# Values of a gated linear attention branch: features on partitions before, tokens on partitions now

## The reference

```
u, q, k, v, r, glr, ga, gb = split(h @ w_in)       # v: 512 columns, 4 heads of 128
q, k, v, r, glr = [to_col_major(t, rows) for ...]  # latent tokens only; rows = 8
# per direction, per chunk of 64 tokens:
kv    = einsum('jd,je->de', k * exp(g_last - gc), v)
state = decay * state + kv
o     = (masked scores) @ v + (q * exp(gc)) @ state_at_chunk_start
```

## Time and profile before

| | us |
|---|---|
| median of 3 runs | 1352.38 |
| profiled execution, its own time | 1354.73 |
| span of its trace | 1353.0 |
| PE busy | 1335.8 (99%) |
| VectorE busy | 864.3 (64%) |
| GpSimd busy | 652.2 (48%) |
| ScalarE busy | 395.8 (29%) |

### The profile page before, as it was taken

The page is one execution under the profiler, slowest core; times in us unless marked ns, Lnnn a source line. Parts: engine busy times, 40 slices in busy tenths (PEclk is TensorE's granted clock), DMA queues, the critical chain, the costliest instruction groups (busy, mean ns, idle before and its releaser), DMA issues.

```text
span 1353.0 us, 21483 instructions
## 1 busy us (share of the span) xinstructions
PE 1335.8 (99%) x8556; PEld 1232.3 (91%) x8556; DVE 864.3 (64%) x1383; ACT 395.8 (29%) x750; POOL 652.2 (48%) x408
## 2 busy tenths in 40 slices
PE   7999999999999999999999999999999999999998
PEld 5899999999999999998888888888998999999997
DVE  5697368468556555537656649926778755555666
ACT  4310010210210110124635321222142555544455
POOL 3164444543543543532732356636567455655554
PEclk9999999999999999999999999999999999999999
DMA  9653354353454344223322479484736233344322
GB/s 319 199 148 91 119 147 125 113 159 115 126 140 134 106 128 152 63 55 109 81 61 51 129 211 260 152 268 145 229 87 199 63 94 94 109 116 114 99 75 82
DMA packets 242798, 178.18 MB, mean 132 GB/s; under 512 B 33288, under 2 KB 219916, under 8 KB 242700
## 3 DMA queue, kind: packets, MB, share of 16 engines
q1 hardware_dynamic: 222640, 145.78, 37.7%
q10 hardware_dynamic: 20060, 31.04, 7.0%
HBM read 156.93 MB, written 19.86 MB: 131 GB/s over the span
## 4 chain that ended last, share of the span: by engine, by line
PE 92%; DVE 4%; ACT 1%; issue 1%; ACTq 0%; DMA 0%; POOL 0%; DVEq 0%; POOLq 0%
PE ps L1276 46%; PE ps L2041 13%; PE ps L1636 13%; PE ps L2100 7%; PE ps L1287 1%; PE ps L1914 1%; DVE ada_acc L2924 1%; DVE ps L3028 1%; PE ps L2127 1%; PE ps L1951 1%; PE ps L1739 1%; PE ps L1531 1%; PE ps L1482 1%; PE ps L1776 1%; ACT squares L2197 0%
## 5 line engine op out<-in xcount | busy, mean ns | idle before, releaser
L1177 POOL TENSOR_SCALAR w_hi<-w_raw 128x1024 fp32r<-128x1024 f32 x128 | 154.7, 1209 | 526.8 <-PE ps L1276 279.4
L1180 POOL TENSOR_TENSOR w_lo<-w_raw,w_hi 128x1024 fp32r<-128x1024 f32 x128 | 325.0, 2539 | 10.7
L1276 PE MATMUL ps<-h_hi,w_lo 128*128 128x384 f32 (+2 forms) x984 | 287.3, 351 | 0.0
L1276 PE MATMUL ps<-h_hi,w_hi 128*128 128x384 f32 (+2 forms) x984 | 283.0, 346 | 0.0
L1276 PE MATMUL ps<-h_lo,w_hi 128*128 128x384 f32 (+2 forms) x984 | 283.0, 346 | 0.0
L1276 PEld LDWEIGHTS ps<-h_hi,w_lo 128*128 128x128 f32 x984 | 175.8, 188 | 14.9 <-issue 4.3
L1276 PEld LDWEIGHTS ps<-h_hi,w_hi 128*128 128x128 f32 x984 | 177.6, 188 | 10.8
L1276 PEld LDWEIGHTS ps<-h_lo,w_hi 128*128 128x128 f32 x984 | 177.8, 188 | 10.4
L1254 POOL TENSOR_TENSOR w_lo<-w_raw,w_hi 128x512 fp32r<-128x512 f32 x90 | 115.8, 1301 | 104.4 <-ACT w_hi L2673 102.9
L2924 DVE SCALAR_TENSOR_TENSOR ada_acc<-ada_w,cs,ada_acc 128x1024 f32<-128x1024 f32 x70 | 114.5, 1671 | 6.0 <-DMA ada_w<-in_ada_w_dram 4.0
L2041 PE MATMUL ps<-h_hi,w_hi 128*128 128x256 f32 x360 | 102.0, 283 | 0.0
(11 more groups left out here) (452 smaller groups left out, 2648.1 us busy)
## 6 DMA issues: line engine op xcount, KB each, us to landing
w_raw<-in_ffn_w_gate_dram SPq DMA_DIRECT2D x44, 512.0 KB, 5.0
w_raw<-in_ffn_w_up_dram SPq DMA_DIRECT2D x44, 512.0 KB, 4.1
w_raw<-in_ffn_w_down_dram SPq DMA_DIRECT2D x44, 512.0 KB, 3.9
ada_w<-in_ada_w_dram ACTq DMA_DIRECT2D x32, 512.0 KB, 3.9
w_raw<-in_w_in_dram SPq DMA_DIRECT2D x32, 512.0 KB, 4.1
ada_w<-in_ada_w_dram SPq DMA_DIRECT2D x24, 512.0 KB, 4.0
ada_q<-in_ada_w_dram SPq DMA_DIRECT2D x8, 1024.0 KB, 10.7
c_scr<-cp ACTq DMA_DIRECT2D x16, 288.0 KB, 3.7
```

Source lines behind the costliest of these rows:

```text
L1177: pool.tensor_scalar(w_hi[:, s, 0:cols], w_raw[:, s, 0:cols], 1.0, 1.0, ALU.mult, ALU.mult)\
L1180: pool.tensor_tensor(w_lo[:, s, 0:cols], w_raw[:, s, 0:cols], w_hi[:, s, 0:cols].bitcast(F32), ALU.subtract).then_inc(w_split, 1)
L1276: last = pe.matmul(mv[2], st, mv[part], start=(first and q == 0), stop=(n == len(terms) - 1 and q == 2))
```

## The change

The 512 columns of the value weights are now cut along the contraction. A unit holds two of the eight blocks and all 512 columns, so its rows are 2 KB long. `values()` holds a 128-token block of `h` stationary and lets 512 weight columns stream: for each of 4 units 6 token blocks, 2 contraction blocks and 3 passes. The six results stay in six PSUM banks (jobs v0 to v2, two banks each) over all four units. They have tokens on partitions already, so `v_t` and the transposes are gone.

The two context blocks are copied by ScalarE straight to `v_sb`. The four latent blocks are copied to `v_row`, in row-major order of the grid. Regrouping them moves tokens between partitions, and SP does it with 32 transfers from `v_row` to `v_sb`: for each grid row r and each quarter t of the grid columns, 16 neighbouring partitions of 512 floats go to every eighth partition of tile t. The first 16 wait for job v0 to be copied, the other 16 for v1. `key_values(0)` waits for all 32 (`v_here`).

The units of the values are now released by a semaphore of their own (`v_ok`), which PE raises once per unit, and once each as the three jobs are complete. Job numbers are padded, so that all later jobs keep their banks. The core of the diff:

```
-              ("v", 4), ("u0", 1), ("vt", 6), ("gla", GLA_JOBS), ...
+              ("v", 3), ("v_pad", 2), ("u0", 1), ("u0_pad", 1), ("gla", GLA_JOBS), ...
...
-    v_t = place("v_t", [P, 4, NT], F32, at=ut_at)
+    v_row = place("v_row", [P, 4, VAL], F32, at=ut_at)
...
+        def values_read(q):
+            return q + 1 if q < 3 else 6
+        def values_made(m):
+            return 4 + m
...
+            def value_unit(q):
+                n = UNIT["v"] + q
+                unit(n, w_in[:, 2 * q:2 * q + 2, C_V:C_V + VAL], raw(n % 4, 2, VAL))
+            def turn_values():
+                for r in range(ROWS):
+                    if r % 4 == 0:
+                        was_read(sp, JOB["v"] + r // 4)
+                    for t in range(4):
+                        w0 = GRID_W * (r % 2) + P // ROWS * t
+                        sp.dma_start(v_sb[r:P:ROWS, t, :], v_row[w0:w0 + P // ROWS, r // 2, :]).then_inc(v_here, 16)
...
-            tall(UNIT["v"], 3, C_V)
+            for q in range(3):
+                value_unit(q)
...
-            tall(UNIT["v"] + 3, 1, C_V + 3 * P)
+            value_unit(3)
             tall(UNIT["u"], 4, C_U)
             for q, t in enumerate(R_ORDER):
+                if q == 3:
+                    turn_values()
                 tall(UNIT["r"] + q, 1, C_R + t * P)
...
             def split(n, cols):
                 pool.wait_ge(w_here[n % 4], 16 * (n // 4 + 1))
-                is_done(pool, last_user(n - 4))
+                q = n - 4 - UNIT["v"]
+                if 0 <= q < 4:
+                    pool.wait_ge(v_ok, values_read(q))
+                else:
+                    is_done(pool, last_user(n - 4))
...
+            def values():
+                for q in range(4):
+                    n = UNIT["v"] + q
+                    wh, wl = [w[:, n % 4, :].rearrange("p (k c) -> p k c", k=2) for w in (w_hi, w_lo)]
+                    pe.wait_ge(w_split, n + 5)
+                    for t in range(6):
+                        j = JOB["v"] + t // 2
+                        if q == 0 and t % 2 == 0:
+                            wait_read(pe, j)
+                        o = (lat, ctx_)[t % 2](j)
+                        for k in range(2):
+                            for r, (h, w) in enumerate(((h_hi, wl), (h_lo, wh), (h_hi, wh))):
+                                last = pe.matmul(o, h[:, 2 * q + k, P * t:P * t + P], w[:, k, :], start=(q == 0 and k == 0 and r == 0),
+                                                 stop=(q == 3 and k == 1 and r == 2))
+                        if t == 5 or (q == 3 and t % 2 == 1):
+                            last.then_inc(v_ok, 1)
...
-            for q in range(4):
-                tall_job("v", q, JOB["v"] + q, NT)
-            input_part(0)
-            for q in range(4):
-                was_read(pe, JOB["v"] + q)
-            for t in range(6):
-                j = JOB["vt"] + t
-                wait_read(pe, j)
-                for q in range(4):
-                    last = transpose(lat(j)[:, P * q:P * q + P], v_t[:, q, P * t:P * t + P])
-                last.then_inc(job_done, 1)
+            values()
+            input_part(0, JOB["gla"] - JOB["v"])
...
             def key_values(p):
+                if p == 0:
+                    pe.wait_ge(v_here, 16 * ROWS * 4)
...
+            def take_v(m):
+                j = JOB["v"] + m
+                act.wait_ge(v_ok, values_made(m))
+                dst = v_row[:, 2 * m:2 * m + 2, :] if m < 2 else v_sb[:, 4:6, :]
+                first = act.activation(dst[:, 0, :], lat(j), ACT.Copy)
+                if m == 2:
+                    first.then_inc(slot_read[(j + 1) % 4], 1)
+                act.activation(dst[:, 1, :], ctx_(j), ACT.Copy).then_inc(slot_read[j % 4], 1 if m == 1 else 2)
...
-            evac_tokens(JOB["v"], v_t[:, 0, :], NT, P)
             decays(0)
-            for q in range(1, 4):
-                evac_tokens(JOB["v"] + q, v_t[:, q, :], NT, P)
+            take_v(0)
+            take_v(1)
             decays(1)
+            take_v(2)
             take_u(0)
-            for t in range(6):
-                take_v(t)
```

More of the change, by code:

```diff
@@ L238 @@
               ("ffn1", FFN1_JOBS), ("norm1", 0), ("q0", 1), ("q1", 1), ("glr", 1), ("k", 2), ("z0", 1), ("z1", 1),
-              ("v", 4), ("u0", 1), ("vt", 6), ("gla", GLA_JOBS), ("chunks", 23), ("gb", 6), ("ga", 8), ("merge", len(MERGE_ORDER)),
+              ("v", 3), ("v_pad", 2), ("u0", 1), ("u0_pad", 1), ("gla", GLA_JOBS), ("chunks", 23), ("gb", 6), ("ga", 8), ("merge", len(MERGE_ORDER)),
               ("ma", KD), ("wo", KD), ("ada7", 1), ("wo_b", 4), ("ffn2", FFN2_JOBS),
@@ L358, in last_user @@
 def last_user(n):
-    for name, count, jobs in (("k", 2, JOB["k"]), ("q0", 1, JOB["q0"]), ("glr", 1, JOB["glr"]), ("q1", 1, JOB["q1"]), ("v", 4, JOB["v"]),
+    for name, count, jobs in (("k", 2, JOB["k"]), ("q0", 1, JOB["q0"]), ("glr", 1, JOB["glr"]), ("q1", 1, JOB["q1"]),
                               ("ga", 8, JOB["ga"]), ("wo", 4, JOB["wo"])):
@@ L803, in build @@
         hc_ok = sem("hc_ok")
+        v_ok = sem("v_ok")
+        v_here = sem("v_here")
         xn_ok = sem("xn_ok")
@@ L1721, in tall_job, with input_part @@
                 split_mm(tall_terms(name, q, j, toks, c)).then_inc(job_done, 1)
-            def input_part(p):
+            def values():
[14 more added lines that the diff above has]
+                            last.then_inc(v_ok, 1)
+            def input_part(p, jobs=1):
                 q, j = p // 2, GJ["u", p]
@@ L1731, in input_part @@
                 split_mm([(wh[:, k, :], wl[:, k, :], [(h_hi[:, k, c], h_lo[:, k, c], lat(j)[:, 0:c.stop - c.start])])
-                          for k in range(KD)]).then_inc(job_done, 1)
+                          for k in range(KD)]).then_inc(job_done, jobs)
             def latents(name, q, j, c, k0, k1):
```

## The result

The changed kernel takes 1361.8 us (median of 6 runs, 1359.98 to 1364.79), the kernel before, run beside it, 1353.99 us (6 runs, 1352.18 to 1355.9). The ratio is 1.0054 with a 95% interval of 1.0041 to 1.0067, so some 7.3 us slower (5.6 to 9.1). The forecast was 1351.4 us and its range ended at 1356.0. The profiled execution of the changed kernel took 1364.79 us for a span of 1363.1.

What follows compares the result with a forecast made beforehand. The prediction took PE (TensorE) as the bound: -0.95 us (fewer, wider matmuls), -2.62 (transposes) and +2.5 (new wait) give -1.0 us, from a median of 1352.38 to 1351.4 us; range 1348.8 to 1356.0, eight times in ten.

Steps and rivals of the forecast that it cites:

- What bounds the kernel: Whole kernel: PE, busy 99% of the span, is the bound; time taken from its row arrives at the end.
- PE's own work: GLA values on PE: 144 matmuls for 192 save 0.95 us, dropped transposes 2.62 us; first v_sb matmul 3.57 us earlier.
- SP's start: SP's queue: the first of the 32 transfers is issued at 682.8 us, behind the r2 load.
- ScalarE's copies: Before the transfers: two copies of tile pair 0 end at about 682.3 us; SP starting late for them would show error.
- The pace of SP's issues: The 32 transfers on SP: issued 0.46 us apart like the u_scr stores, the last issued at 697.1 us.
- a hiccup: Among the 32 SP issues: a delay of 1.2 us might be shared, and a quarter of it was added.
- PE's new wait: Before the first v_sb matmul: PE waits about 2.5 us for the transfers, so 1.0 us of 3.57 is kept.
- What is queued behind: Behind the transfers on SP: the r3 load comes 6 us later but has 50 us to spare.
- C: Rival, chance 0.15: the 32 issues on SP become the bound of this stretch; 1356.3 us, with slow landings 1358.1.
- B: Rival, chance 0.13: SP issues 0.38 us apart or less, so PE's wait is hidden; 1348.8 us, at best 1348.4.
- D: Rival, chance 0.08: the microsecond won is lost again where VectorE ends last (1006 to 1050 us); 1352.4 us.
- The doubt whether many small transfers may take the place of transposes: The 32 KB transfers: a skill rule calls those under 64 KB mostly overhead; 14.3 us of issuing against 2.62 of transposes.

Runs made afterwards that it cites:

- e5_noturn: Changed kernel without any regrouping: ScalarE copies all tiles straight to v_sb, no transfers, no wait; 1351.51 us, ratio 0.9977 to the kernel before.
- e7_queue_only: Changed kernel without regrouping; the 32 transfers go to an unread DRAM buffer and key_values(0) does not wait for them; 1350.32 us, ratio 0.9969 to the kernel before.
- e2_todram: Changed kernel without regrouping; the 32 transfers go from v_sb to an unread DRAM buffer and PE still waits for them; one run of 1355.03 us.
- e6_halves: Changed kernel with each of the 32 transfers cut into two of 256 floats per row, 64 in all, same result; one run of 1382.61 us.
- e1_contig: Changed kernel with each transfer writing 16 neighbouring partitions instead of every eighth, so tokens are not regrouped; one run of 1364.34 us.
- e8_fill: Changed kernel with the u2 job (24 matmuls, 5.5 us) moved in front of key_values(0); 1356.07 us, ratio 1.0013 to the kernel before.
- e4_bounce: Changed kernel regrouping through DRAM with two 512 KB stores and four 256 KB loads instead of 32 transfers; 1352.41 us, ratio 0.9979 to the kernel before.

## Why the prediction was wrong

**What bounds the kernel** held. PE is the chain, and what is added to its row before 800 us arrives at the end.

**PE's own work** held, with a term a little small. The 144 matmuls take from 655.68 to 688.50, 32.82 us or 227.9 ns each, so 1.19 us are saved and not 0.95. The forecast named the Trainium skill's N/2.4 + 2.5 ns here, but the same section ("TensorE: Matmul & The Clock Gate", "Back-to-back issue gap") gives it for an isolated matmul and has about 131 ns at 512 columns for a stream with weight loads. This trace bears out neither: 227.9 ns. The forecast's term came from rows, so nothing of it hung on that. The transposes are gone. PE would be at the first `v_sb` matmul at 698.90, 3.81 us earlier than before, where the forecast had 3.57; e5_noturn and e7_queue_only confirm it with 3.90.

**SP's start** was 0.6 us late. In times of the trace before, the first issue comes at 685.77 - 2.37 = 683.4 and not 682.8. The r2 load in front of it waited for GpSimd's split of u2, whose first half took 1.88 us and not 1.05. It is 1.87 or 1.88 us in all nine traces with the new values, so it comes with the change; why was not looked into:

```profile
680.66 1.88 POOL L1202 TENSOR_SCALAR w_hi<-w_raw 128x1024 fp32r<-128x1024 f32 x1 [4.08 <-PE ps L1765]
682.63 2.71 POOL L1205 TENSOR_TENSOR w_lo<-w_raw,w_hi 128x1024 fp32r<-128x1024 f32 x1
```

ScalarE's copies, named as a danger, were no part of it: tile pair 0 was copied between 683.26 and 684.34, before SP turned to it.

**The pace of SP's issues** is the step that failed. The forecast took 0.46 us from the stores to DRAM because they also have 16 partitions, and set the 0.63 us of the earlier trace rows aside as the upper bound, since those read short pieces out of DRAM. It chose by the shape of the transfer. What counted was the memory at its ends: the same rows go to DRAM at 0.468 (e2_todram) and to the scratchpad at 0.632, whatever the bytes (e6_halves) and the step of the partitions (e1_contig). The forecast had said that no trace shows a transfer from scratchpad to scratchpad, and had named issues further apart than 0.5 us as a sign that it is wrong. 31 gaps at 0.17 us more are 5.3 us. With 0.6 us for the start and 0.1 for the landing (2.0 and not 1.9 us), less the 0.3 us allowed for a hiccup that did not come, it is 5.7 us; `key_values(0)` missed the forecast's 699.3 by 5.8 (707.44 - 2.37 = 705.07).

**The granted clock** is the second thing that failed: it was missing in the sum altogether. The forecast named PE's new wait of 2.5 us, but priced it as 2.5 us. All six kernels in the table that wait for 3.1 us or more paid 1.6 to 2.7 us on top. A fall behind a shorter wait is on record, but in thinner work: in the start-up of the changed kernel's trace PE waits 2.3 us until 28.16 us, between other short waits, and the granted clock is 0.78 from 29 to 30 us and 0.50 from 30 to 31. Whether a wait of 2.5 us in dense work would have done so isn't known; if it had, the forecast's own -1.0 us would have been a loss of about 1 us.

**What is queued behind** held: e7_queue_only holds SP for 16 us and the changed kernel for 20.2 us, and nothing behind them is lost.

**The rivals.** C happened, with its mechanism, its place and its pace of 0.63 us, and was given 0.15. The pace came from loads out of DRAM, another kind of transfer, so that it fits to 0.01 us is in part luck. Its price of +3.9 us was short of the clock: its v_sb time of 704.2 against 705.07 measured, and then 2.2 us more make 1352.4 + 4.7 + 2.2 = 1359.3, which is the ratio of 1.0054 (1352.38 x 1.0054 = 1359.7) within its interval. B and D fell. The doubt whether many small transfers may take the place of transposes was right in kind, as the Trainium skill has it in "DMA: Bandwidth & Descriptors", "Rules for kernel authors": small ones should be made into one. The runs agree: six large transfers need 13.2 us where 32 small ones need 21.6, and of the kernels tried that do all the work only the one with six is faster than before. The forecast used that rule only to weigh landings against issues, and kept the slower pace for its bounds.

## What to carry to other kernels

Price many small transfers by issue time multiplied by their number, and take that issue time from a row with the same kinds of ends (scratchpad or DRAM), not with the same shape. If the trace has no such row, as here, the slowest pace among the small transfers belongs in the middle of the forecast and not at its edge. If the number decides, fewer and larger transfers can win even when every byte moves twice. And a wait put on TensorE where it never stood still can cost more than its length: look at the granted clock behind it.

## What the runs showed of the hardware

- One issue on SP's queue: 589 ns (0.632 us apart) from scratchpad to scratchpad, the same for 32 KB and 16 KB and for neighbouring or stepped partitions; 420 ns (0.468 us apart) for the same rows from scratchpad to DRAM; and 420 ns (0.457 us apart) for the `gate_up` loads of 16 KB from DRAM to scratchpad. But it is 598 ns for the four regrouping loads of e4_bounce from DRAM to scratchpad, 585 for the k_scr loads of the earlier trace rows and 368 for the unit loads of the earlier trace rows, so the kind of ends is not all that counts. What else makes the difference was not settled.
- ScalarE's queue issues such a transfer in 611 ns, beside SP's, which stay at 590 ns.
- After PE's waits of 3.1 to 28.8 us the granted clock was down to 0.50, the 1.2 GHz level (0.57 over 4 us in e8_fill), at a price of 1.6 to 2.7 us that did not grow with the wait and that the windows behind it account for within 0.2 us.
- Single issues can be long (1427 ns in e8_fill, 1617 ns in the earlier trace rows, 2024 ns in the earlier trace rows). What they have in common isn't known.
